# A hybrid Mamba-2 / sparse-attention layer on one core: block means by column quarters with a second product, and the order of work ahead of the convolution's projection

## The reference, cut to what matters

```python
def block_means(rows):
    B, L = rows.shape[:2]
    r = rows.reshape(B, L // CMP_BLOCK, CMP_BLOCK, 2, KV_HEADS, HEAD_DIM)
    return jnp.mean(r.astype(jnp.float32), axis=2).astype(rows.dtype)
...
    kv_c = block_means(kv_c_rows)
```

## Time and profile before

| | us |
|---|---|
| median of 3 runs | 985.8 |
| lowest and highest run | 982.7, 985.88 |
| the profiled execution's own time | 985.73 |
| its span, first to last instruction | 983.9 |
| PE matmul busy | 924.6 (94%) |
| DVE busy | 490.6 (50%) |
| ACT busy | 343.1 (35%) |
| POOL busy | 158.8 (16%) |
| mean granted clock of PE | 0.978 |

### The profile page before, as it was taken

The page is one execution under the profiler, slowest core; times in us unless marked ns, Lnnn a source line. Parts: engine busy times, 40 slices in busy tenths (PEclk is TensorE's granted clock), DMA queues, the critical chain, the costliest instruction groups (busy, mean ns, idle before and its releaser), DMA issues.

```text
span 983.9 us, 13227 instructions
## 1 busy us (share of the span) xinstructions
PE 924.6 (94%) x5187; PEld 573.6 (58%) x5187; DVE 490.6 (50%) x961; ACT 343.1 (35%) x698; POOL 158.8 (16%) x125
## 2 busy tenths in 40 slices
PE   2999999999999999997989888899999999999995
PEld 1454764465566567776555545556666666666762
DVE  1141301135353445558623445886767666676553
ACT  3140000201011224443132334675665546544531
POOL 1003491000000144435211000900000000000000
PEclk9999999979999989998999999999999999999998
DMA  8926435123120000300832134400000000011011
GB/s 280 352 75 258 171 123 204 44 84 114 57 87 1 5 1 1 86 1 1 310 133 92 47 127 149 129 2 22 12 23 23 22 23 23 1 44 44 1 44 65
DMA packets 36567, 80.67 MB, mean 82 GB/s; under 512 B 3044, under 2 KB 17580, under 8 KB 35162
## 3 DMA queue, kind: packets, MB, share of 16 engines
q1 hardware_dynamic: 32010, 49.39, 15.1%
q0 software_dynamic: 4496, 30.44, 8.6%
HBM read 69.64 MB, written 14.30 MB: 85 GB/s over the span
## 4 chain that ended last, share of the span: by engine, by line
PE 77%; DVE 9%; ACT 5%; issue 4%; DMA 4%; SPq 1%; POOL 0%; ACTq 0%; DVEq 0%
PE PS L1615 12%; PE PS L1554 12%; PE PS L1861 11%; PE PS L1901 7%; PE PS L1924 6%; PE PS L1946 6%; PE PS L1523 3%; PE PS L1597 3%; DMA U<-in_cache_slc_kv,idx 2%; PE PS L1473 1%; PE PS L1783 1%; DMA W<-in_w_ada 1%; PE PS L1558 1%; DVE T L1211 1%; PE PS L1809 1%
## 5 line engine op out<-in xcount | busy, mean ns | idle before, releaser
L1615 PE MATMUL PS<-hT,W 128*128 128x363 f32 (+1 forms) x384 | 119.9, 473 | 0.0
L1597 PE MATMUL PS<-W,hT 128*128 128x512 f32 x256 | 113.0, 594 | 0.0
L977 ACT ACTIVATE T<-PS,small 128x640 f32<-128x640 f32 (+7 forms) x128 | 88.7, 706 | 53.6 <-DVE small L1411 53.3
L1615 PEld LDWEIGHTS PS<-hT,W 128*128 128x128 f32 x384 | 73.2, 192 | 46.6 <-issue 3.0
L1411 DVE TENSOR_REDUCE small<-PS 128x1 f32<-128x640 f32 (+7 forms) x86 | 81.8, 971 | 31.8 <-PE PS L1915 31.3
L1554 PE MATMUL PS<-W,hT 128*128 128x288 f32 (+1 forms) x256 | 86.5, 500 | 0.0
L1924 PEld LDWEIGHTS PS<-consts,T 128*128 128x128 f32 x544 | 60.7, 141 | 35.2 <-issue 32.9
L1924 PE MATMUL PS<-consts,T 128*128 128x128 f32 x544 | 79.6, 276 | 1.5 <-ACT hT L1001 1.5
L1597 PEld LDWEIGHTS PS<-W,hT 128*128 128x128 f32 x256 | 48.2, 191 | 54.7 <-issue 54.1
L1554 PEld LDWEIGHTS PS<-W,hT 128*128 128x128 f32 x256 | 48.5, 190 | 37.4 <-issue 30.7
L1861 PE MATMUL PS<-U,Y 128*128 128x512 f32 x128 | 60.5, 599 | 2.4 <-DVE Q L1434 1.3
(11 more groups left out here) (415 smaller groups left out, 1566.3 us busy)
## 6 DMA issues: line engine op xcount, KB each, us to landing
W<-in_w_in SPq DMA_DIRECT2D x5, 2048.0 KB, 9.1
W<-in_w_ada SPq DMA_DIRECT2D x8, 1024.0 KB, 11.5
U<-in_x_prompt SPq DMA_DIRECT2D x8, 512.0 KB, 8.0
W<-in_w_ada SPq DMA_DIRECT2D x2, 2048.0 KB, 8.0
U<-in_state_win_kv POOLq DMA_DIRECT2D x8, 512.0 KB, 5.0
hT<-in_x_prompt SPq DMA_DIRECT2D x8, 512.0 KB, 3.9
out_y_prompt<-hT SPq DMA_DIRECT2D x8, 512.0 KB, 3.1
out_new_win_sample<-in_state_win_kv POOLq DMA_DIRECT2D x1, 4032.0 KB, 22.2
```

The costliest lines, as they stand in the source:

```text
L977: ins = act.activation(Pb[u % 4][:, m * step:m * step + n * P], S[:, m, :], ACT.Exp, bias=sneg_m[u % 2][:, m:m + 1], accum_out=dsum[i % 2] ...
L1597: ins = nc.tensor.matmul(bank(z_bank(u)), hT3[:, k, i * P:(i + 1) * P], w, start=(k == 0), stop=(k == KT8 - 1))
L1615: ins = nc.tensor.matmul(bank(b, 0, n), w[:, k, ct % 4 * P:ct % 4 * P + P], hT3[:, k, a:a + n], start=(k == 0), stop=(k == KT8 - 1))
```

## The change

The block means are computed with the operands swapped: the constant `blk`, now a sliding table of 60 columns, is the stationary operand (32 columns for each token tile), and the tokens' 256 columns of keys and values are the moving one. Token tile i goes to the column quarter i % 4, two tiles add up in each, and the result in bank 3 is 128 rows (quarter by block) of 256 columns. ACT copies it to SBUF (`block_parts`). A second product with the constant `fold` (one where row mod 32 is the block) adds the four quarters: four matmuls on the four column quarters give the values, already in the layout that `Vbd` needs, and one gives the keys, transposed; all in bank 7. DVE no longer copies block keys and values between the two steps. The products now stand ahead of the samples' key transposes, and PE's waits for DVE's copies stand inside the convolution's projection: ahead of the third token part of `ct` 0 and 1, and ahead of the gate sums. The constant `sel` becomes the first 9 columns of `fold`. `KcT` shrinks from 160 to 32 columns, the table of constants grows from 2,023 to 2,102 columns. In the diff, `act`, `nc.vector` and `nc.tensor` name the engine.

```diff
-    parts["sel"] = ((p[:, None] % 32 == np.arange(9)[None, :])).astype(f)
+    parts["fold"] = ((p[:, None] % 32 == np.arange(NCB)[None, :])).astype(f)
...
-    parts["blk"] = (p[:, None] // CB == np.arange(P // CB)[None, :]).astype(f) / f(CB)
+    parts["blk"] = (p[:, None] // CB == np.arange(-28, 32)[None, :]).astype(f) * (np.arange(-28, 32)[None, :] < P // CB) / f(CB)
...
+        block_parts = U[:, 8448:8704]
...
+            act.wait_ge(s_blocks, 1)
+            act.activation(block_parts, bank(3, 0, 256), ACT.Copy).then_inc(s_blocks_out, 1)
...
             nc.vector.tensor_copy(KnT[:, :], bank(4, 0, 128)).then_inc(s_keys_out, 1)
-            nc.vector.tensor_copy(KcT[:, 0:NCB], bank(4, 128, 160))
-            nc.vector.tensor_copy(KcT[:, NCB:].rearrange("p (h c) -> p h c", h=GQ),
-                                  bank(4, 160, 192).unsqueeze(1).broadcast_to([P, GQ, NCB])).then_inc(s_keys_out, 1)
             nc.vector.tensor_copy(KcTs[:, :], bank(5, 0, 256)).then_inc(s_keys_out, 1)
...
             dve.wait_ge(s_cmp_values, 1)
+            nc.vector.tensor_copy(KcT[:, :], bank(7, 128, 160)).then_inc(s_keys_out, 1)
...
+            pe.wait_ge(s_kv_evac, 13)
+            for i in range(TT):
+                j = i % 4
+                ins = nc.tensor.matmul(bank(3, 0, 256)[32 * j:32 * j + 32], const("blk")[:, 28 - 4 * i:60 - 4 * i], kvc3[:, i, :],
+                                       start=(i < 4), stop=(i >= 4))
+            ins.then_inc(s_blocks, 1)
             pe.wait_ge(s_keys_out_act, 2)
             pe.wait_ge(s_keys_out, 2)
-            pe.wait_ge(s_kv_evac, 13)
...
-            for i in range(TT):
-                for a in range(2):
-                    nc.tensor.matmul(bank(4, 128 + a * 32 + 4 * i, 132 + a * 32 + 4 * i), kvc3[:, i, a * P:(a + 1) * P], const("blk"),
-                                     start=True, stop=True)
...
-            pe.wait_ge(s_keys_out, 6)
-            nc.tensor.matmul(bank(6, 0, P), KcT[:, NCB:], ident, start=True, stop=True).then_inc(s_cmp_values, 1)
+            pe.wait_ge(s_blocks_out, 1)
+            for h in range(GQ):
+                nc.tensor.matmul(bank(7, 0, P)[32 * h:32 * h + 32], const("fold"), block_parts[:, P:], start=True, stop=True)
+            nc.tensor.matmul(bank(7, P, P + NCB), block_parts[:, 0:P], const("fold"), start=True, stop=True).then_inc(s_cmp_values, 1)
...
                 for b, a, n in X_PARTS[ct % 2]:
+                    if ct < 2 and b >= 4:
+                        pe.wait_ge(s_keys_out, 5)
...
                 if ct in (1, 2):
                     pe.wait_ge(s_mod_copied, 4 + ct)
+                    pe.wait_ge(s_keys_out, 7)
...
                 if ct in (0, 1):
-                    if ct == 0:
-                        pe.wait_ge(s_keys_out, 7)
                     mod_group(4 + ct, G_GATE + ct, 6)
```

More of the change, by code:

```diff
@@ L89, in constants @@
     parts["cm"] = cm.reshape(P, TT * NCB)
-    parts["blk"] = (p[:, None] // CB == np.arange(P // CB)[None, :]).astype(f) / f(CB)
+    parts["blk"] = (p[:, None] // CB == np.arange(-28, 32)[None, :]).astype(f) * (np.arange(-28, 32)[None, :] < P // CB) / f(CB)
+    parts["blk"] = parts["blk"].astype(f)
     s = np.arange(P)
@@ L158, in build_layer @@
         KnT = sb("KnT", 2 * SR)
-        KcT = sb("KcT", 5 * NCB)
+        KcT = sb("KcT", NCB)
         Vbd = sb("Vbd", KVH * GQ * HD)
@@ L171, in build_layer @@
         ident = const("ident")
+        sel = const("fold")[:, 0:9]
         cosT = const("cos").rearrange("p (i f) -> p i f", f=HR)
@@ L226, in build_layer @@
         s_act_chain = sem('act_chain')
+        s_blocks = sem('blocks')
+        s_blocks_out = sem('blocks_out')
         s_blocksum = sem('blocksum')
@@ L1142, in _ @@
                 q = slice(32 * h, 32 * h + 32)
-                ins = nc.vector.tensor_copy(Vbd4[q, :, h, :], bank(6, 0, 128)[q].rearrange("p (k d) -> p k d", k=KVH))
+                ins = nc.vector.tensor_copy(Vbd4[q, :, h, :], bank(7, 0, 128)[q].rearrange("p (k d) -> p k d", k=KVH))
             ins.then_inc(s_keys_out, 1)
@@ L1487, in mod_sum @@
                     a = 160 + 36 * p + 9 * c
-                    ins = nc.tensor.matmul(bank(7, a, a + 9), modc[p % 2][:, c * P:(c + 1) * P], const("sel"), start=True, stop=True)
+                    ins = nc.tensor.matmul(bank(7, a, a + 9), modc[p % 2][:, c * P:(c + 1) * P], sel, start=True, stop=True)
                 ins.then_inc(s_mod_summed, 1)
@@ L1622, in _ @@
                     pe.wait_ge(s_gate_rows, ct - 1) if ct > 1 else None
-                    nc.tensor.matmul(bank(7)[0:9], const("sel"), modc[1 + ct], start=True, stop=True).then_inc(s_mod_summed, 1)
+                    nc.tensor.matmul(bank(7)[0:9], sel, modc[1 + ct], start=True, stop=True).then_inc(s_mod_summed, 1)
                 if ct in (0, 1):
-                    if ct == 0:
-                        pe.wait_ge(s_keys_out, 7)
                     mod_group(4 + ct, G_GATE + ct, 6)
@@ L1963, in _ @@
             sp.dma_start(Y[1:9, 0:1024], A["c_sample"]).then_inc(s_c_in, 16)
-            early = where["sel"][0] + where["sel"][1]
+            early = where["fold"][0] + where["fold"][1]
             sp.dma_start(consts[:, 0:early], A["table"][:, 0:early]).then_inc(s_ident_in, 16)
```

## The result

The changed kernel takes 971.68 us (median of 4 executions, 969.61 to 974.39), the kernel before 985.12 us on the same count (982.7 to 985.88). The ratio is 0.9876, with a 95% interval from 0.9848 to 0.9905: 13.4 us less where 8.4 were forecast, and under the range, which ended at 973.9. With the later executions of both kernels (105 before, 15 changed) the means are 983.7 and 972.3 us, 11.4 us less, still under the range. The profiled execution took 972.79 us, its span is 971.0, the mean granted clock 0.987 in place of 0.978.

A forecast was written before the change was run, and what follows sets the result against it. PE was taken to bound the kernel, busy 924.6 of 983.9 us. An earlier projection (7.10 us) and the held clock (1.31) gave 8.41 us: 985.73 - 8.41 = 977.3 us, range 973.9 to 981.2.

The forecast's parts named there:

- The path: From the end of the key transposes to the projection's start: 3.01 us in place of 10.11, so 7.10 us earlier.
- block product: Block means in the new form, 16 records of 256 moving columns on column quarters: 0.99 us, bounds 0.93 and 3.43.
- compressed means: The two compressed-mean transposes on PE ahead of the projection: 0.25 us at 2.4 GHz, 0.53 at the lower clock.
- state transposes: Eight convolution-state transposes on PE ahead of the second product: 0.71 us at the full clock, 0.99 at the lower.
- ACT's copy: ACT's new 128x256 copy between the two products: 0.38 us, costed at nothing because 1.27 us of PE transposes cover it.
- The clock at this place: The clock holds at 2.4 GHz into the convolution's projection, so its first 48 records cost 14.83 us, 1.31 us less.
- rival (a): The clock falls at the edited place anyway, the projection's 1.31 us are not gained: 979.3 us, chance 0.18.
- The step that failed: Everything behind the edited place slides earlier with PE, with no further gain or loss added to the 8.41 us.
- Rival (b): Later clock falls move in the sample pairs: one vanishes (974.4 us) or one is added (980.2 us), chance 0.17.
- Rival (c): The column quarters do not share the array in the two new products: 2.95 us back, 980.3 us, chance 0.04.
- Rival (d): A later wait, only the gate weight being found as candidate, takes up the gain: 985 us, chance 0.05.
- Rival (e): Slower: clock low as the projection begins and falling in all three pairs that keep it now: 988.1 us, chance 0.02.

## Why the prediction was wrong

**The path.** 7.10 us forecast; 10.11 - 2.93 = 7.18 measured. Step by step: block product 0.99, measured 1.00; sample keys 0.31 and 0.27; compressed means 0.25 and 0.37; state transposes 0.71 and 0.60; second product 0.35 and 0.36; key product 0.40 and 0.34. ACT's copy 0.38 and 0.39, covered by 0.8 us. All right. Two of the terms were off by some 0.1 us, the compressed means too low and the state transposes too high, and cancelled. What the sum did not say is how much of the 7.1 was the clock already: at the full clock the old products take 3.55 us and not 5.40, and what is saved in work and waits is 4.4.

**The clock at this place.** 1.31 us forecast, 16.14 - 14.72 = 1.42 measured. Right, and rival (a), that transposes would let it fall, is out: no profile of a kernel with the new form (ten of them) shows a fall between 196 and 215 us, except the one with the old products added. Even 1.52 us of waiting did not bring it down.

**The step that failed** is the one sentence that "What follows is released by PE or by things that PE released, so I let all of it slide". It put the clock behind the edited place at nothing. The work did slide; the clock did not. The fall at 343 us was left out of the sum as if it belonged to the sums' idle time, wherever that stands. The runs show that it hangs on how far this idle time begins behind the last rise, and that the old form, by its fall at 200 us, had put it at a bad distance in both profiles of the kernel before. Without that fall it is gone in the changed kernel's profile, though not in every kernel with the new form. In the two profiles compared above it is worth 3.03 us. On average the clock gives 7.0 us, of which (8.59 - 4.4) = 4.2 lie at the edited place, where the forecast had them in its 8.41, and 2.8 behind it, where it had nothing. That is nearly all of the 3.0 us between the mean gain of 11.4 and the forecast. Of the profiled executions' 12.9 us, the 1.9 that were not followed are as much a part of the miss, and what made them stays open. The other 2 us of the 13.4 first measured did not last over more executions.

**Rival (b)** had the mechanism, a later fall that moves, and for one fall a price (2.92 us) near what the sums show. But it was laid out for the sample pairs alone, and as a toss between a gain and a loss. The profile before held a better reading: two falls within 150 us of each other, one at the edit and one behind it with little but dense, fixed work between, which is the case in which the second can hang on the first. I listed the first among the rows and not the second. A range down to 973.9 took in one vanished fall and nothing for a second part. In the pairs themselves the profiles did not agree: one of the changed kernel has a fall in the second pair, at 501.18, another has none.

**Rival (c)** is refuted: 1.00 us in quarters, 3.57 in one. **Rival (d)**: no wait of PE took the gain; in the projection PE waited neither for the gate weights nor for DVE. **Rival (e)**: no execution of the changed kernel came above 976.35 us.

What stays open: whether the two products ahead of the sums made the changed kernel slower at all (its half clock was 4 us higher, within the spread), and which of the later falls hang on which. Only the pair at 200 and 343 us was taken apart.

## What to carry to other kernels

A stretch of tiny products on PE cost twice here: once by its own length, and once by the clock that fell with it, at the place and, in the kernel before, where the next light stretch stands. Price both, and read every fall in the trace as a chain: if only dense work lies between two falls, ask whether the second would be there without the first. The matmuls with few moving columns and a full stationary operand were worth turning over, with the large side moving and the small side spread over the column quarters, although that needed a second product to fold them: 1.00 + 0.36 + 0.34 us, where the old products took 3.55 at the full clock.

## What the runs showed of the hardware that was not expected

The kernel before became faster by 5.2 us on average when 1.72 us of useless dense work was put into an idle time of 1.47 us. And its mean time did not rise (mean -1.2 and -0.8 us) with 0.86 or 1.72 us of useless work in the middle of a dense stretch, while 3.43 us cost their full price (+3.7). For such a kernel, differences of some 3 us between two versions can be the clock's alone, so each time wants its mean clock beside it: by 105 executions, 10 us at half clock cost 4.4 us.
